# Selected-block attention stage: another slab order, compressions mixed one to one with projection parts, output slabs split later

## What is computed

```python
z = h @ w_in                       # 1024 query columns, 6 x 128 key/value columns, 48 gate columns
q, kv_c, kv_s, kv_w, g = split(z)  # compressed, selected, window keys and values
gates = sigmoid(g + gate_b)
def compress(t, pe, w1, w2):       # blocks of 32 tokens, stride 16: 15 blocks
    blk = t[:, cidx] + pe[:, None, :]
    return silu(blk @ w1) @ w2     # w1 is 2048 x 128, w2 is 128 x 64
k_cmp = compress(kv_c[:, :, 0], ...);  v_cmp = compress(kv_c[:, :, 1], ...)
# per query block: attention over the compressed blocks, over selected blocks, over a window
o = gates[0] * o_c + gates[1] * o_s + gates[2] * o_w
y = o @ w_out                      # 1024 x 1024
```

## The kernel before

| place | 0 | 1 | 2 | 3 | 4 | 5 | 6 | 7 | 8 | 9 to 11 | 12 to 15 |
|---|---|---|---|---|---|---|---|---|---|---|---|
| before | comp. keys | comp. values | sel. keys | w1 keys | window keys | gates | queries 0 | w1 values | values | queries 1 to 3 | output |
| after | comp. keys | comp. values | sel. keys | window keys | w1 keys | gates | queries 0 | w1 values | values | queries 1 to 3 | output |

## Time and profile before

### The profile page before, as it was taken

One profiled execution on the slowest core, in us unless ns is written; L12 is line 12 of the kernel. 1 busy time (PEld: TensorE's weight loads), 2 busy tenths in 40 slices (PEclk: granted clock), 3 DMA queues, 4 the chain that ended last, 5 costly groups with the idle time before them and its releaser, 6 DMA issues.

```text
span 2343.4 us, 41745 instructions
## 1 busy us (share of the span) xinstructions
PE 2220.8 (95%) x17489; PEld 2157.5 (92%) x17489; DVE 1526.4 (65%) x2066; ACT 963.7 (41%) x1259; POOL 104.0 (4%) x54
## 2 busy tenths in 40 slices
PE   7999879999999999999999998889999999979998
PEld 6999768999999998899999997779999998969998
DVE  5777765777777646665465558967557556576555
ACT  3433433433533445443354343134435344544333
POOL 0000000000000000000000003610000000000000
PEclk9999887999999979999999999999999999989999
DMA  7776432777677431165445552214553553323552
GB/s 305 304 288 268 166 124 89 281 278 276 242 298 291 146 142 73 37 233 180 180 143 198 179 176 77 104 57 167 177 195 144 181 179 143 144 90 124 182 181 87
DMA packets 52940, 417.57 MB, mean 178 GB/s; under 512 B 5872, under 2 KB 6000, under 8 KB 6768
## 3 DMA queue, kind: packets, MB, share of 16 engines
q1 hardware_dynamic: 52848, 416.27, 48.0%
HBM read 415.20 MB, written 1.05 MB: 178 GB/s over the span
## 4 chain that ended last, share of the span: by engine, by line
PE 80%; DVE 14%; ACT 3%; issue 1%; DMA 1%; POOL 0%; DVEq 0%; SPq 0%; ACTq 0%
PE AB L272 15%; PE AB L273 15%; PE AB L274 15%; PE Y L272 9%; PE Y L273 9%; PE Y L274 9%; DVE lo L1639 3%; DVE qT L2354 2%; PE M L588 2%; PE M L541 1%; ACT hi L1173 1%; DMA ada_raw<-ada 1%; DVE ada_acc L1675 1%; PE Y L813 1%; PE N L854 1%
## 5 line engine op out<-in xcount | busy, mean ns | idle before, releaser
L1639 DVE TENSOR_TENSOR lo<-raw,hi 128x2048 fp32r<-128x2048 f32 x310 | 721.6, 2328 | 492.6 <-ACT hi L1173 492.5
L272 PE MATMUL AB<-h_hi,hi 128*128 128x256 f32 x3040 | 877.0, 288 | 14.1 <-DVE ada_raw L2364 5.7
L273 PE MATMUL AB<-h_lo,hi 128*128 128x256 f32 x3040 | 866.6, 285 | 0.0
L274 PE MATMUL AB<-h_hi,lo 128*128 128x256 f32 x3040 | 866.4, 285 | 0.0
L1173 ACT ACTIVATE hi<-raw 128x2048 fp32r<-128x2048 f32 x322 | 614.0, 1909 | 525.8 <-PE Y L274 278.6
L272 PEld LDWEIGHTS AB<-h_hi,hi 128*128 128x128 f32 x3040 | 589.9, 194 | 19.3 <-DVE ada_raw L2364 6.8
L273 PEld LDWEIGHTS AB<-h_lo,hi 128*128 128x128 f32 x3040 | 590.1, 194 | 0.2
L274 PEld LDWEIGHTS AB<-h_hi,lo 128*128 128x128 f32 x3040 | 589.9, 194 | 0.0
L272 PE MATMUL Y<-g_hi,hi 128*128 128x256 f32 x1280 | 362.2, 283 | 0.0
L273 PE MATMUL Y<-g_lo,hi 128*128 128x256 f32 x1280 | 362.2, 283 | 0.0
L274 PE MATMUL Y<-g_hi,lo 128*128 128x256 f32 x1280 | 362.2, 283 | 0.0
(11 more groups left out here) (341 smaller groups left out, 2258.6 us busy)
## 6 DMA issues: line engine op xcount, KB each, us to landing
raw<-slabs SPq DMA_DIRECT2D x322, 1024.0 KB, 4.8
ada_raw<-ada SPq DMA_DIRECT2D x35, 2048.0 KB, 8.1
kT<-ada SPq DMA_DIRECT2D x1, 1024.0 KB, 10.6
vt<-ada SPq DMA_DIRECT2D x1, 1024.0 KB, 12.6
x<-x_t SPq DMA_DIRECT2D x1, 1024.0 KB, 14.6
out_t<-x SPq DMA_DIRECT2D x4, 256.0 KB, 2.4
vec<-vectors SPq DMA_DIRECT2D x1, 462.0 KB, 4.1
hf<-constants SPq DMA_DIRECT2D x1, 401.0 KB, 14.6
```

The costliest lines, as they stand in the source:

```text
L272: nc.tensor.matmul(out_, w_hi, r_hi, start=start, stop=False, **kw)
L273: nc.tensor.matmul(out_, w_hi, r_lo, start=False, stop=False, **kw)
L274: return nc.tensor.matmul(out_, w_lo, r_hi, start=False, stop=stop, **kw)
L1639: nc.vector.tensor_tensor(lo[slot][:, :], raw[slot][:, :], hi[slot][:, :].bitcast(F32), ALU.subtract).then_inc(lo_done[slot], 1)
```

## The change

`NSA_SLABS` swaps places 3 and 4, so the window keys come ahead of the first compression's weights. PE does eight parts of the window keys with nothing between them, then the first compression one step to one part (the other eight window-key parts, then the eight parts of the gates). Queries 0: six parts, the gate transposes, the wait for the second compression's slab (`held["c"] = slab()`), six more parts, and then the second compression one step to one part (the last four query parts, then twelve of the sixteen value parts), and the last four value parts alone. ACT and DVE split the slabs in that order: place 3 ahead of the first block copies, and DVE's `block_low(0)` stands behind the `lo` of place 4. Later, places 10 to 12 are split beside attention groups 3, 11 and 19 on ACT (4, 12 and 20 on DVE), where before place 10 was split ahead of attention (DVE: beside group 0) and places 11 to 13 beside groups 1, 9 and 17 (2, 10 and 18); place 13 is now split after attention, as places 14 and 15 are.

```diff
-        NSA_SLABS = [4, 5, 6, 10, 7, 9, 0, 11, 8, 1, 2, 3, 12, 13, 14, 15]
+        NSA_SLABS = [4, 5, 6, 7, 10, 9, 0, 11, 8, 1, 2, 3, 12, 13, 14, 15]
...
-                    w_hi, w_lo, done = slab()
+                    w_hi, w_lo, done = held["c"] if kv else slab()
...
-                def window_keys(j):
-                    if j == 3:
-                        held["w"], held["outs"] = slab(), halves(result("a"))
-                    if j >= 3:
-                        parts(held["w"], held["outs"], range(3 * (j - 3) // 2, 3 * (j - 2) // 2) if j < 13 else
-                              range(15, 16) if j == 13 else ())
-
-                compressed(0, window_keys)
-
-                w_hi, w_lo, done = slab()
-                for k in range(KD):
+                held["w"], held["outs"] = slab(), halves(result("a"))
+                parts(held["w"], held["outs"], range(KD))
+
+                def gate_part(k):
+                    if k == 0:
+                        held["g"] = slab()
+                    w_hi, w_lo, done = held["g"]
                     at = k * 2 * P
                     mm = mm3(y_bank(2)[0:48, 0:T], ...)
...
+                compressed(0, lambda j: parts(held["w"], held["outs"], [KD + j]) if j < KD else gate_part(j - KD))
 
                 held["w"], held["outs"] = slab(), halves(result("a"))
                 keys_read["q", 0] = c["read_a"]
-                parts(held["w"], held["outs"], range(KD))
+                parts(held["w"], held["outs"], range(6))
                 pe.wait_ge(gate_copied, 1)
...
-                compressed(1, lambda j: parts(held["w"], held["outs"], [KD + j // 2] if j % 2 else ()))
-
-                tokens(halves(result("d")), 2 * P)
+                held["c"] = slab()
+
+                def token_part(i):
+                    if i == 0:
+                        held["v"], held["vouts"] = slab(), halves(result("d"))
+                    w_hi, w_lo, done = held["v"]
+                    t, k = divmod(i, KD)
+                    mm = mm3(held["vouts"][t], ...)
+                    if i == 2 * KD - 1:
+                        mm.then_inc(done, 1)
+
+                parts(held["w"], held["outs"], range(6, 12))
+                compressed(1, lambda j: parts(held["w"], held["outs"], [12 + j]) if j < 4 else token_part(j - 4))
+                for i in range(12, 2 * KD):
+                    token_part(i)
...
# ACT
                     ready(kv)
+                    if kv == 0:
+                        next_slab()
...
-                    next_slab()
+                    if kv == 0:
+                        next_slab()
+                for kv in range(2):
                     act.wait_ge(blk_ready, kv + 1)
...
                 keys(0, 2)
                 next_slab()
-                ready(3)
+                keys(1, 3)
+                next_slab()
+                ready(4)
                 nc.scalar.activation(hid[:, :], M[:, 0:2 * NCMP], ACT.Silu).then_inc(hid_ready, 1)
-                next_slab()
-                keys(1, 4)
-                next_slab()
                 ready(5)
                 nc.scalar.activation(gate_rows, ...)
+                next_slab()
                 next_slab()
...
                 nc.scalar.activation(eps_[:, 1:2], eps_[:, 0:1], ACT.Exp)
-                next_slab()
...
-                beside.update({1: next_slab, 9: next_slab, 17: next_slab})
+                beside.update({3: next_slab, 11: next_slab, 19: next_slab})
...
                 turn_pair(3)
+                next_slab()
                 next_slab()
...
# DVE
+                def block_low(kv):
+                    dve.wait_ge(cmp_hi, kv + 1)
+                    th, tl = ((g_hi, g_lo), (z_hi, z_lo))[kv]
+                    nc.vector.tensor_tensor(tl[:, 0:32 * NCMP], blocks[kv], ...).then_inc(cmp_in, 1)
+
                 for kv in range(2):
+                    next_slab()
+                    if kv:
+                        block_low(0)
                     dve.wait_ge(cmp_copied, kv + 1)
...
-                    next_slab()
-                    dve.wait_ge(cmp_hi, kv + 1)
...
+                block_low(1)
...
                     ins.then_inc(read_dve, 1)
                     c.take("read_d")
-                    next_slab()
...
-                beside = {2: next_slab, 10: next_slab, 18: next_slab}
+                beside = {4: next_slab, 12: next_slab, 20: next_slab}
...
                 turn_pair(3)
+                next_slab()
```

More of the change, by code:

```diff
@@ L959, in nsa @@
                              k == 0, k == KD - 1)
-                mm.then_inc(done, 1)
+                    if k == KD - 1:
+                        mm.then_inc(done, 1)
+                compressed(0, lambda j: parts(held["w"], held["outs"], [KD + j]) if j < KD else gate_part(j - KD))
                 held["w"], held["outs"] = slab(), halves(result("a"))
                 keys_read["q", 0] = c["read_a"]
-                parts(held["w"], held["outs"], range(KD))
+                parts(held["w"], held["outs"], range(6))
                 pe.wait_ge(gate_copied, 1)
@@ L969, in nsa @@
                 mm.then_inc(gate_turned, 1)
-                compressed(1, lambda j: parts(held["w"], held["outs"], [KD + j // 2] if j % 2 else ()))
-                tokens(halves(result("d")), 2 * P)
+                held["c"] = slab()
[4 more added lines that the diff above has]
+                    t, k = divmod(i, KD)
+                    mm = mm3(held["vouts"][t], h_hi[:, k, t * P:(t + 1) * P], h_lo[:, k, t * P:(t + 1) * P],
+                             w_hi[:, k * 2 * P:(k + 1) * 2 * P], w_lo[:, k * 2 * P:(k + 1) * 2 * P],
+                             k == 0, k == KD - 1)
+                    if i == 2 * KD - 1:
+                        mm.then_inc(done, 1)
+                parts(held["w"], held["outs"], range(6, 12))
+                compressed(1, lambda j: parts(held["w"], held["outs"], [12 + j]) if j < 4 else token_part(j - 4))
+                for i in range(12, 2 * KD):
+                    token_part(i)
                 all_but_queries = c["read_d"]
@@ L2245, in nsa @@
                     next_slab()
+                def block_low(kv):
+                    dve.wait_ge(cmp_hi, kv + 1)
+                    th, tl = ((g_hi, g_lo), (z_hi, z_lo))[kv]
+                    nc.vector.tensor_tensor(tl[:, 0:32 * NCMP], blocks[kv], th[:, 0:32 * NCMP].bitcast(F32),
+                                            ALU.subtract).then_inc(cmp_in, 1)
                 for kv in range(2):
+                    next_slab()
+                    if kv:
+                        block_low(0)
                     dve.wait_ge(cmp_copied, kv + 1)
@@ L2257, in nsa @@
                     ins.then_inc(blk_ready, 1)
-                    next_slab()
-                    dve.wait_ge(cmp_hi, kv + 1)
-                    th, tl = ((g_hi, g_lo), (z_hi, z_lo))[kv]
-                    nc.vector.tensor_tensor(tl[:, 0:32 * NCMP], blocks[kv], th[:, 0:32 * NCMP].bitcast(F32),
-                                            ALU.subtract).then_inc(cmp_in, 1)
+                block_low(1)
                 c.take("res", 3)
```

## The result

| | before | after |
|---|---|---|
| median | 2340.43 us (4 runs, 2338.93 to 2342.05) | 2319.53 us (4 runs, 2318.98 to 2319.91) |
| span of the profiled execution | 2343.4 | 2317.7 |
| mean granted clock | 0.965 | 0.978 |

The ratio of the times is 0.991, 95% interval 0.9893 to 0.9928: 20.9 us faster. Timed again beside the experiments, the kernel before had medians of 2338.3 to 2340.8 us and the changed one 2319.3, so the gain is 19 to 21.5 us.

A forecast was written before the change was run, and what follows sets the result against it. PE was taken as the bound, busy at half clock in the front part. Gains of 11.1 there and 0.9 in attention made 12.0 us: 2333.4 profiled, 2329.5 for the median; range 2324 to 2339.5.

The forecast's parts named there:

- Direction and mechanism of the front: From 833.2 us to the first score: PE busy at half clock; dense runs and one-to-one mixing would keep full clock.
- both new waits: PE waits 2.4 us for place 7 before the second compression, and 3.3 us for DVE's value copy before the first score.
- Front part: From 833.2 us to the first score: first score at 871.6 instead of 882.7, 11.1 us gained with the waits taken off.
- hidden detail: Start of the first compression: its slab and `cmp_in`, ready at about 835.1, would be covered by eight window-key parts until 836.1.
- My argument from the mix: Both compressions: one step to one part, 48 long of 96 matmuls without waits, holds full clock; otherwise up to 11.9 us lost.
- +0.9: Attention: net gain in us from moving the slab splits, 2.1 gained less 1.2 lost, clock falls summing to zero.
- The first term: Attention's start: place 10's `lo` no longer stands between DVE's first and second maximum, 2.1 us gained.
- The rival in which attention gains more: Attention: moved splits wholly covered and both clock falls vanish, 5 us more gained, 2324.5 us; chance 0.10.
- After attention: Behind attention: place 13's split and the next feed-forward's first slab DMA stay hidden, the latter with 3 us to spare.
- The cold attention: Attention: the clock falls in the wait before the first score and stays down, 13.7 us a round; chance 0.06.
- the fallen compressions: Clock falls in the second compression, 2339.2 us, chance 0.13; or in both because one to one fails, 2341.5, chance 0.08.
- my recorded estimate: Compression pairs at half clock: with a clock-independent weight load a pair would cost 0.95 us in place of 1.25.

The follow-up runs named there:

- splits only: The kernel before with only the slab splits moved: places 10 to 12 beside groups 3, 11, 19, place 13 after attention; median 2331.5 us, ratio 0.9967.

## Why the prediction was wrong

**Direction and mechanism of the front: right.** The clock in the front part was the largest gain, 11.9 of the 17.8 to 19.4 us in the stage, and both new waits came where they were worked out.

**Front part: right.** 11.1 forecast, 11.9 measured. Pairs cost 0.69 us for 0.71, those with gates 0.62, and the waits 0.60, 2.11 and 3.33 us for 0.2, 2.4 and 3.3. That the eight parts ahead of the first compression cover the wait for its operands, which I had entered as a hidden detail, is what the whole 11.9 hangs on: without them the first compression fell at one to one as with the old mix. My argument from the mix was half the reason.

**Attention: the step that failed.** "+0.9" was 2.1 for the split between the first two maxima and -0.4 for each moved split. Measured: 4.0 in round 1, 0.9 in rounds 2 and 3. The first term stood on the wrong split, which was free. The second split's 2.40 us of idle time stood in my own rows as the upper bound, and I had taken 0.4 lost for it, without a row that says so. I had called both places of each split equal in kind. They are not: at group 1 the `lo` and the wait for its `hi` stand ahead of the first `pT` copy, for which PE stood 3.71 us before. In full the two moved splits are worth 5.6 us in round 1 (23.2 to 17.6 in "splits only"), of which the fall of the clock that the 3.3 us wait now brings takes 1.6 back (19.3 with it, 17.6 and 17.7 in the two versions without). The rival in which attention gains more, at 5 us more and with a chance of 0.10, counted this split's 2.40 us, but also the 2.1 that was free and a fall of the clock that stayed; that its sum is near the 4.0 us that my term fell short by is luck.

**After attention: right in that nothing waits.** The tail went from 56.9 to 56.0 and 54.3, which I had left at equal. The clock was down for 10.2 us at the end of attention in both profiles of the kernel before, and for 6.8 and 3.4 in the changed one's. That is 0.9 to 2.6 us more; whether place 13's later split causes it is not shown.

**Range.** 11.9 + 4.0 + 0.9 and 0.9 to 2.6 make 17.8 to 19.4 us in the stage, and the medians differ by 19 to 21.5. The remainder of some 2 us lies in stages that the change doesn't touch; the profiles there scatter by up to 10 us, and the two of the kernel before are the highest. Versions with the change reach the same times in those stages, so it may be chance; whether they do so less often stays open. The cold attention and the fallen compressions did not come.

**The weight load and the clock.** The run without the dense stretch repeats that short matmuls, weight load and all, cost about twice as much at half clock. Two steps of its first compression, with one part between them:

```profile
832.87 0.23 PE L272 MATMUL M<-g_hi,hi 128*128 128x30 f32 x1
...
834.15 0.23 PE L272 MATMUL M<-g_hi,hi 128*128 128x30 f32 x1
```

A pair takes 1.28 us there against 0.69 in the changed kernel, and 13 of them in a row 16.6 us. Three long matmuls alone, in the gates behind them, take 0.64 us, so three short ones take 0.64 too, against 0.33 at full clock (0.69 less 3 x 0.119). The Trainium skill ("TensorE: Matmul & The Clock Gate", section "LDWEIGHTS (loading the stationary operand)") gives a weight load a time that doesn't depend on the clock, and by my recorded estimate from it a pair would cost 0.95; the runs here don't agree, and the measurement decides. One reading in the prediction was wrong: of the 98 matmuls before, not half but about a third were short (33 of the 96 in the timeline). The disagreement holds without it, by the pairs above, in which half are.

## What to carry to other kernels

Where a slow stretch is full and its granted clock is half, look for the wait ahead of it, not only at what is in it: a wait of 2 us straight ahead of thin work went with a front 12 us longer here, and 24 long matmuls moved into that wait bought the 12 us back. A slab split written between other work costs what stands behind it in that engine's order plus its own wait, so price the place, not the work: the same 1.9 and 2.3 us were free at one place and cost 3.3 us and more two groups earlier, with another split close ahead. And when work gets faster, look for the next in-order wait: one that needs nothing from the instruction ahead of it can be swapped with it, 3 us for two exchanged lines.

## What the hardware showed that I had not expected

A mix of two short steps to one long part held 2.4 GHz for 6.7 us behind a dense run and then fell, while the denser one-to-one mix that begins behind a wait of 2.14 us fell after 1.7 us and then ran its last 17.6 us at 1.2 GHz without coming back; it came back in the gates, which have long rows alone. Where the clock falls in one and the same code differs from execution to execution: 0.54 or 0.72 over the same 30 us of the first attention, and 158.4 to 164.5 us between the same two slab splits around it.
